# Query tiles' memory as a seventh place for gathered rows, and memory scores in three pieces

## What is computed

```
for each layer:
    mixer:   z = modulate(x) @ w_in, split into pool | q, kv (low rank) | memory q, k, v, gates
             attention: 8 heads, q = rms_norm(zq) @ w_uq, k, v = rms_norm(zkv) @ w_ukv
             memory, 4 heads, 2 directions: h = (q k^T * exp(gate terms)) v / max(|den|, exp(-m))
             x += gate * concat(pool, attention, memory) @ w_out
    PEER:    for each token: q = h @ w_q (8 heads x 2 halves of 128)
             s = q . subkeys  -> top 16 of 128 for both halves -> top 16 of the 256 sums
             g = softmax(best);  a = gelu(h . u_tab[expert])
             x += gate * sum over 8 x 16 experts of (g * a) * v_tab[expert]
context tokens pass only through the first layer's PEER; in layer 2 they give keys and values alone
```

## Time and profile before

| | us |
|---|---|
| median of 3 runs | 2786.68 |
| lowest, highest | 2786.67, 2791.87 |
| the profiled execution | 2789.06 |
| its span, first to last instruction | 2787.3 |

### The profile page before, as it was taken

How to read it: one execution, slowest core, us unless ns; L and a number is a source line. 1 busy time by engine, 2 the same in 40 slices (tenths; PEclk the granted TensorE clock), 3 DMA queues, 4 the chain that set the end, 5 groups by cost and what they waited for, 6 DMA issues and landing times.

```text
span 2787.3 us, 26625 instructions
## 1 busy us (share of the span) xinstructions
PE 2209.2 (79%) x8372; PEld 1037.6 (37%) x8372; DVE 1639.0 (59%) x4029; ACT 1121.3 (40%) x3259; POOL 813.1 (29%) x772
## 2 busy tenths in 40 slices
PE   7979899776777787787677777786799987777776
PEld 4747555332344343343122111175575321221111
DVE  2143567658786644676777666431525667776654
ACT  3132353545663433355333333332423343333333
POOL 0000233333354322334434333200003444343331
PEclk9869999778899889898899999995799999999999
DMA  7631599979999999999999999910016999999997
GB/s 316 235 123 36 217 404 406 358 275 393 395 387 421 421 420 421 412 420 421 422 421 421 421 421 421 372 71 30 16 37 242 424 425 426 425 426 426 426 426 309
DMA packets 133660, 940.05 MB, mean 337 GB/s; under 512 B 14864, under 2 KB 16144, under 8 KB 23312
## 3 DMA queue, kind: packets, MB, share of 16 engines
q0 software_dynamic: 110592, 805.36, 70.0%
q1 hardware_dynamic: 22496, 130.31, 11.9%
q10 hardware_dynamic: 432, 2.70, 0.3%
HBM read 937.26 MB, written 1.05 MB: 337 GB/s over the span
## 4 chain that ended last, share of the span: by engine, by line
DMA 45%; PE 31%; DVE 10%; ACT 10%; issue 3%; POOL 1%; SPq 0%; DVEq 0%; POOLq 0%; ACTq 0%
DMA fast<-uv_dram,idx 28%; DMA mix<-uv_dram,idx 16%; PE bank L1744 10%; PE bank L1703 4%; PE bank L1481 4%; DVE fast L1346 3%; PE bank L1667 2%; PE bank L1559 2%; ACT diag L921 1%; PE bank L1475 1%; ACT coef L918 1%; PE bank L1537 1%; PE bank L1651 1%; PE bank L1712 1%; ACT L917 1%
## 5 line engine op out<-in xcount | busy, mean ns | idle before, releaser
L1744 PE MATMUL bank<-fast,diag 128*64 128x512 f32 x2024 | 802.6, 664 | 294.5 <-ACT diag L921 292.7
L619 POOL DMA_INDIRECT fast<-uv_dram,idx x506 | 544.2, 1075 | 1497.5 <-PE bank L1744 778.5
L1346 DVE SCALAR_TENSOR_TENSOR fast<-fast,hrow 128x1024 f32<-128x1024 f32 x506 | 619.3, 1225 | 407.7 <-DMA fast<-uv_dram,idx 401.2
L917 ACT ACTIVATE gact<-araw 128x1 f32<-128x1 f32 x768 | 154.8, 202 | 1024.0 <-DVE fast L1346 645.0
L1744 PE MATMUL bank<-mix,diag 128*64 128x512 f32 x820 | 387.9, 630 | 120.9 <-ACT diag L921 119.3
L1744 PEld LDWEIGHTS bank<-fast,diag 128*64 128x64 f32 x2024 | 191.3, 145 | 762.0 <-ACT diag L921 513.6
L1346 DVE SCALAR_TENSOR_TENSOR mix<-mix,hrow 128x1024 f32<-128x1024 f32 x205 | 251.4, 1226 | 194.7 <-DMA mix<-uv_dram,idx 192.3
L619 POOL DMA_INDIRECT mix<-uv_dram,idx x205 | 206.4, 1007 | 327.5 <-PE bank L1744 306.1
L921 ACT ACTIVATE diag<-con,coef 128x64 f32<-128x64 f32 x768 | 267.1, 348 | 25.1
L918 ACT ACTIVATE coef<-gact,wts 128x1 f32<-128x1 f32 x768 | 226.2, 295 | 24.9
L1744 PEld LDWEIGHTS bank<-mix,diag 128*64 128x64 f32 x820 | 93.7, 140 | 370.0 <-ACT diag L921 250.3
(11 more groups left out here) (231 smaller groups left out, 2601.3 us busy)
## 6 DMA issues: line engine op xcount, KB each, us to landing
fast<-w_dram SPq DMA_DIRECT2D x48, 1024.0 KB, 7.2
back<-w_dram SPq DMA_DIRECT2D x44, 1024.0 KB, 10.4
qring<-wq_dram SPq DMA_DIRECT2D x40, 576.0 KB, 8.6
fast<-uv_dram,idx POOLq DMA_INDIRECT x506, 19.6
mix<-wq_dram SPq DMA_DIRECT2D x8, 576.0 KB, 6.3
mix<-uv_dram,idx POOLq DMA_INDIRECT x205, 26.3
fast<-uq_dram SPq DMA_DIRECT2D x4, 576.0 KB, 4.0
xT<-x_dram ACTq DMA_DIRECT2D x1, 2048.0 KB, 9.1
```

What stands on the lines that cost most here:

```text
L619: g.indirect_dma_start(slot(e, m), None, uv_tabs[e], bass.IndirectOffsetOnAxis(idx[:, Q % 2, n:n + 1], 0)).then_inc(landed[place], 16)
L917: link(a.activation(gact[:, n:n + 1], araw[:, Q % 2, n:n + 1], ACT.Gelu))
L1346: v.scalar_tensor_tensor(out=u, in0=u, scalar=1.0, in1=hrow[:, (2 * i + half) % 3, :], op0=ALU.mult, op1=ALU.mult, accum_out=araw[:, Q % 2 ...
L1744: mm = t_.matmul(acc[half, f * 512:(f + 1) * 512], diag[:, j % DIAGS, :], slot(e, j)[:, D + f * 512:D + (f + 1) * 512], start=(j % SLOTS < ...
```

## The change

Three edits:

1. A seventh place, `query`: the first 2048 columns of `qring`. It is open for slots 52 to 195, and its first gather waits for the key scores of units 0 to 15 (`psc_mm`). Units 16 and 17 are loaded at slot 196 instead of 41 and 49, after slot 195's values.
2. A memory unit's work on TensorE comes in three pieces. The gates' spreads and `st_mm` stay at slot 63 + 7h and wait, from the second unit on, for the exponentials of the unit before (`mE_ready`) instead of its weighting. The scores of the first two chunks come at +1, behind `mP_ready`, those of the other two at +2. A new signal `sc_mem` follows them, and VectorE's weighting of e = 0 waits for it.
3. The query norm's third square and its sum come two slots later (ScalarE at 45, TensorE at 47), and mean, root and scaling two slots later too (48, 49, 50).

```diff
-USES = (FAST_USES[0] + [("ctx", 0, 134, 266, "turned"), ("ctx", 0, 312, 512, "projected"),
+USES = (FAST_USES[0] + [("query", 0, 52, 196, "queried"), ("ctx", 0, 134, 266, "turned"), ("ctx", 0, 312, 512, "projected"),
...
+QUERY_FREE = 196
...
                 at = 10000 * e + ASKED[e][u - 2] + 2
+                if u in (HC, HC + 1):
+                    at = QUERY_FREE
...
+            if region == "query":
+                return qring[:, :, :, :].rearrange("p b k c -> p (b k c)")[:, 0:BIG]
...
+            if what == "queried":
+                return psc_mm, psc_mm.at(0, HC)
...
                     elif u >= 8:
+                        if u == HC:
+                            sp.wait_ge(v_used.sem, v_used.at(e, freed(e, QUERY_FREE - 1)))
                         sp.wait_ge(psc_mm.sem, psc_mm.at(e, u - 1))
...
                     for k in range(3):
+                        if k == 2:
+                            yield at + 3
                         square(p, KC + 2 + k, zqT[:, k, :])
-                    yield at + 5
+                    yield at + 7
                     root(p, 3)
...
-                    yield at + 4
+                    yield at + 6
                     mean(p, 3, KC + 5, QRANK)
-                    yield at + 6
+                    yield at + 8
                     inverse(p, 3)
...
                         v.wait_ge(mE_ready.sem, mE_ready.at(p, h + 1))
+                        if e == 0:
+                            v.wait_ge(sc_mem.sem, sc_mem.at(p, h + 1))
...
                     for k in range(3):
+                        if k == 2:
+                            yield in_at(group_of(p, "zq", 2) - 1) + 8
                         sum_square(p, KC + 2 + k, k == 0, k == 2)
...
             def memory_scores(p):
                 for h in range(MH):
-                    yield ML_AT + ML_STEP * h
+                    at = ML_AT + ML_STEP * h
+                    yield at
...
                     else:
-                        t_.wait_ge(mP_ready.sem, mP_ready.at(p, 2 * h))
-                    for kc in range(chunks(p)):
-                        mk = mkc if kc >= 2 or PHASES[p][1] else mkx
-                        t_.matmul(bank[kc // 2][:, kc % 2 * SEQ:kc % 2 * SEQ + SEQ], mk[f, c, kc % 2 * P:kc % 2 * P + P], mqT[f, c, :],
-                                  start=True, stop=True)
+                        t_.wait_ge(mE_ready.sem, mE_ready.at(p, h))
                     for e in range(DIRS):
...
                     mm.then_inc(st_mm.sem, 1)
+                    for j in range(chunks(p) // 2):
+                        yield at + 1 + j
+                        if h and j == 0:
+                            t_.wait_ge(mP_ready.sem, mP_ready.at(p, 2 * h))
+                        mk = mkc if j or PHASES[p][1] else mkx
+                        for kc in range(2):
+                            mm = t_.matmul(bank[j][:, kc * SEQ:kc * SEQ + SEQ], mk[f, c, kc * P:kc * P + P], mqT[f, c, :], start=True, stop=True)
+                    mm.then_inc(sc_mem.sem, 1)
```

More of the change, by code:

```diff
@@ L480, in build @@
         st_mm, marg_ready, mE_ready = signal("st_mm", *when(MH)), signal("marg_ready", *when(MH)), signal("mE_ready", *when(MH))
-        mP_ready = signal("mP_ready", *when(2 * MH))
+        mP_ready, sc_mem = signal("mP_ready", *when(2 * MH)), signal("sc_mem", *when(MH))
         num_mm, num_evac = signal("num_mm", *when(MH)), signal("num_evac", *when(MH))
```

## The result

The median of 4 runs is 2750.11 us (2737.53 to 2753.52), against 2789.0 (2786.67 to 2791.87) for the kernel before beside it: ratio 0.9852, 95% interval 0.9819 to 0.9885, 41 us of 2789. The direction was as forecast; the size is nearly twice the 21.1 us of the sum. A second set of 5 runs gave 2743.68 (2740.47 to 2753.2), ratio 0.9858 (0.9837 to 0.988).

The account below looks back on a forecast made before the run. Gather transfers were taken as the bound, with 51 us idle between 400 and 820 us. Terms 9.6 + 0.9 + 3.6 + 4.5 + 2.5 - 0 - 0 = 21.1 us off 2786.7 gave 2766 us, range 2750 to 2780.

Parts of the forecast that it names:

- A microsecond taken from that idle time moves every later gather: Idle transfer time in 400 to 820 us, 51 us in all: any saved is kept, since later gathers run at full rate.
- The pieces behind the experts: Four memory units, 510 to 615 us: with the spread first, the scores leave the chain, saving 9.6 us (5 to 11.3).
- The place: Seventh gather place: one more megabyte under way, worth 3.6 after unit 3, 4.5 in 615 to 745 us, 2.5 of run-ahead.
- the waits of the first slots after unit 3 for gathers gone: Sign expected in the changed profile; seven places would save 3.6 us (0 to 4.3) at slots 92 and 93.
- nothing of its own: In the memory units the chain holds no gather, so the seventh place alone gives nothing, only keeping gather waits off.
- the row stage: Stretch of 615 to 745 us: the place recovers half of 9.0 us idle transfer time, 4.5 us (0 to 9.0).
- the run-ahead behind it: After the attention, 745 to 820 us: transfers run one slot further ahead before the full-rate stretch, 2.5 us once (0 to 2.5).
- The queries' price: Loads of queries 16 and 17 move 2.8 us of transfers from 400 to 510 us into the full-rate stretch: taken as 0.
- The 0.9 us of the query norm: Moving the query's third square removes ScalarE's wait for TensorE's sums; worth 0 to 0.9 us, taken as 0.9.
- The place does little: Rival: where engines set the pace a free place gives nothing; 2 to 12 us gained, some 2779 us; chance 0.2.
- The clock comes back: Rival: in 510 to 615 us shorter waits keep TensorE at 2.4 GHz; 10 us more gained, 2756 us; chance 0.15.
- The clock goes: Rival: TensorE's grant falls to 0.66 in the attention and 400 to 510 us; 28 us slower, 2815 us; chance 0.04.

Follow-up runs that it names:

- pieces_m3: Memory scores in three pieces in mixer 3 alone, against the kernel before: 2776.43 us, ratio 0.9951.
- double_open: The changed kernel plus a second buffer for the odd units' masked scores in mixers 0 and 3: 2736.52 us, ratio 0.9828 to the kernel before.
- spread_first_unsplit: The changed kernel, but the scores follow the gates' spread in the same slot, not split: 2771.6 us, ratio 0.9953 to the kernel before.
- late_queries: The kernel before with queries 16 and 17 loaded after slot 195, their memory not used as a place: 2791.01 us, ratio 1.0022.
- zq_only: The kernel before with only the query norm's third square two slots later: 2788.38 us, ratio 1.0014.
- place_to_180: The changed kernel with the seventh place given back and the two queries loaded at slot 180, not 196: 2748.41 us, ratio 0.9871 to the kernel before.
- pieces_only: Memory scores in three pieces in mixers 0, 1 and 3, six places, query norm unchanged, against the kernel before: 2759.37 us, ratio 0.9897.
- pieces_m1: Memory scores in three pieces in mixer 1 alone, six places, against the kernel before: 2777.22 us, ratio 0.9959.
- place_pieces_m1: Seventh place, late query loads and pieces in mixer 1 only, query norm unchanged, against the kernel before: 2764.93 us, ratio 0.9922.
- no_zq: The changed kernel with the query norm as before, so place and pieces alone: 2745.44 us, ratio 0.9858 to the kernel before.

## Why the prediction was right and wrong

**The step that failed is the scope of the first part.** The prediction looks for the wait that counts "In 510 to 615 us, the four memory units", and costs the pieces for these, mixer 1's, alone; the sum has no term for mixers 0 and 3. The chain of mixer 3 would have given it by the same reading as the earlier trace rows: 3.71 us three times and 2.00 once, 13.1 us, and on a chain where nothing else competes. Measured: 12.9 us in the pair of traces, 13.7 by `pieces_m3`, and in the means of the traces 302.4 us for six kernels with the pieces in mixer 3 (`double_open` apart) against 315.9 for six without (`spread_first_unsplit` apart). Mixer 0 has the same code; the three together give 28.7 us, the two single ones 11.4 and 13.7, so it has 3.6 by difference, which the intervals don't separate from nothing. The traces lean the same way: the first dot comes at 310.0 us on average (307.1 to 312.5) in the seven kernels without pieces in mixer 0, and at 305.4 in the six with them (`spread_first_unsplit`, 306.0, apart). But these scatter from 301.5 to 313.4, and the 313.4 is after's own, so its trace shows 2.6 us lost where the others show a gain. The table of stretches was what misled: I looked for idle transfer time, and in mixers 0 and 3 there are hardly any transfers to be idle. "A microsecond taken from that idle time moves every later gather" was right, and so is its counterpart, which I did not ask: where no gather runs, what does the edit touch?

**The second failure is one of size, between slots 0 and 511.** The pair of traces gives 28.2 us there, and it isn't one odd execution: the four kernels without place and without pieces in mixer 1 (before, `pieces_m3`, `late_queries`, `zq_only`) take 1496.4 to 1502.3 us, the six with both take 1467.6 to 1471.7. The place alone takes 1480.5, the pieces 1484.7 and 1487.9: 18.1 and 12.3 us under the mean of neither, and both together 28.6. So nothing shows that one part strengthens the other, though the place alone is a single trace. By stretch, means or single values, with the range in brackets:

| us | neither | place | pieces | both | neither less both | forecast |
|---|---|---|---|---|---|---|
| 0 to 62 | 200.3 | 194.9 | 200.0, 199.6 | 197.7 (194.4 to 200.9) | 2.6 | 0.9 |
| 62 to 92 | 106.3 (102.7 to 109.0) | 99.7 | 93.5, 93.5 | 86.6 (84.7 to 88.5) | 19.7 | 9.6 + 3.6 |
| 92 to 128 | 107.6 (105.2 to 108.8) | 101.3 | 111.1, 108.1 | 101.8 (101.6 to 102.3) | 5.8 | 4.5 |
| 128 to 164 | 98.7 | 98.8 | 99.1, 99.1 | 99.1 | -0.3 | 0 |
| 164 to 196 | 89.9 | 87.5 | 89.8, 90.4 | 87.0 | 2.8 | 2.5 |
| 196 to 224 | 95.9 | 98.8 | 96.4, 95.2 | 98.8 | -2.9 | 0 |
| 224 to 511 | 799.2 | 799.5 | 798.0, 798.7 | 798.9 | 0.3 | 0 |

(`place_to_180` is left out of the rows of 164 and 196 under both, `late_queries` out of that of 196 under neither; under pieces stand `pieces_only` and `pieces_m1`.) The differences add up to 28 us. By the ratios the same two parts, with the pieces in mixer 1 only, give 21.7 us with an interval of 14 to 30, so the runs' times alone would not have shown this.

*The pieces behind the experts*: forecast 9.6 (5 to 11.3), measured 11.4 (8 to 15) by the ratios and 12.6 from the dot of slot 62 to that of 91 (next table). The forecast term holds the scores alone; what it leaves out is the level of the other instructions. Half a unit's numerators (14 instructions) take 1.78 us at the high level and 3.25 at the low one. The first six of the eight halves add up to 14.1 to 16.6 us in the four kernels with neither, 13.9 with the place alone, and 10.7 to 12.1 in all with pieces in mixer 1 (the last two halves are at the high level in all). From the mean of 15.2 to the 11.1 of `pieces_m1` that is 4.1 us, enough for the 3.0 that lie between 12.6 and 9.6; what of it was on the path wasn't isolated, so this cause is argued and not shown.

*The place*: forecast 10.6 in three terms, measured 7.8 (3 to 13) by the ratios, with the loads' cost in it. The border at slot 92 in the table above falls into a wait for a gather, and flatters the place in the row ahead of it: from the dot of slot 91 to that of 92 the kernels with six places take 5.1 to 5.5 us and those with seven about 1.1, but part of this comes back at the next dot, 3.4 to 4.1 against 4.1 to 4.6. VectorE still waits after unit 3 in after, one slot later: 3.11 us at slot 93 and 1.91 at slot 94, where before has 4.29 and 2.40 at slots 92 and 93.

```profile
600.13 1.23 DVE L1359 SCALAR_TENSOR_TENSOR fast<-fast,hrow 128x1024 f32<-128x1024 f32 x1 [3.11 <-DMA fast<-uv_dram,idx]
603.88 1.30 DVE L1359 SCALAR_TENSOR_TENSOR qring<-qring,hrow 128x1024 f32<-128x1024 f32 x1 [1.91 <-DMA qring<-uv_dram,idx]
```

So "the waits of the first slots after unit 3 for gathers gone" did not come true. With the borders at slots 91 and 96 the same kernels give:

| us | neither | place | pieces | both | neither less both | forecast |
|---|---|---|---|---|---|---|
| 62 to 91, the units | 100.9 (97.3 to 103.6) | 98.6 | 88.3, 88.4 | 85.5 (83.6 to 87.4) | 15.4 | 9.6 |
| 91 to 96 | 17.5 (17.2 to 17.9) | 14.3 | 16.8, 16.4 | 14.3 (13.9 to 14.8) | 3.2 | 3.6 |
| 96 to 128 | 95.6 (93.5 to 96.9) | 88.2 | 99.5, 96.8 | 88.7 (88.3 to 89.3) | 6.9 | 4.5 |

In the units the place alone stays within the scatter of neither, as the prediction's "nothing of its own" says; beside the pieces it brings 2.8 us there, as VectorE's waits for gathers shrink (22.4 us in `pieces_m1`, 9.6 + 3.4 in `place_pieces_m1`). Most of the excess over the forecast lies in this row, 15.4 us for 9.6. After unit 3 it brings the forecast amount. In the row stage it brings some 7 us, where the forecast took half of the 9.0 idle ones. The attention stretch doesn't move, and the run-ahead behind it is there, 2.8 for 2.5; both as the absence of gathers in the earlier trace rows said.

**The queries' price was mis-sized.** Taken as 0, bound 2.8; the loads cost 2.9 us in slots 196 to 224 (95.9 to 98.8 in the table), and `late_queries` is 6 us slower (2 to 11). My reason was that the 2.8 us they free in 400 to 510 us might be used there; in the trace that stretch moves at 406 GB/s, for 411 in the earlier trace rows, and `late_queries` takes 200.4 us from slot 0 to 62, where the other three with neither part take 200.0 to 200.5, so they were not. No wait of TensorE took the place: waits for query tiles from 880 to 1100 us are

```profile
PE bank L1723 <- DMA qring<-wq_dram: 3.5, 3, 1.7
```

in after and

```profile
PE bank L1703 <- DMA qring<-wq_dram: 4.2, 3, 1.7
```

in before. Gather 52 went out at 473.4 us, 0.7 later than in the earlier trace rows, and 1.8 earlier counted from each trace's first dot; it kept within the bound of 2.2. The 0.9 us of the query norm can't be seen: `zq_only` is 1.0014 (0.9997 to 1.003), and after is the same with and without it. That VectorE or the transfers end the stretch, and not TensorE's 0.90 us of waiting in the earlier trace rows, would explain it; no run tested it.

**The rivals.** "The place does little" fell: beside the pieces it brings 10 us by the ratios (11.4 to 21.7 with the pieces in mixer 1, and 28.7 to 39.6 from `pieces_only` to `no_zq`). "The clock comes back" came true in a small part. The grant of 510 to 615 us rose from 0.66 to 0.76 (in 510 to 596 us, up to slot 92, after has 0.75, its second execution 0.84, and the other kernels with both parts 0.71 to 0.80), and the numerators went to the high level as told; the values did not all follow: the pair at 527.67 us in after still takes 3.68, behind a wait of 5.14 us for ScalarE, and such waits were the argument against this rival. It was priced at 10 us for a full return; what the traces show of it are the 4.1 us of numerators above, of which it is open how much lay on the path. The rule in the Trainium skill ("TensorE: Matmul & The Clock Gate", HAM oscillation), that closing waits between bursts keeps the array fast, agrees with these numerators (3.25 to 1.78 us); with mixer 3 it doesn't, as the last section shows. "The clock goes" did not happen: 0.96, 0.90 and 0.98 for 0.98, 0.84 and 1.00.

**The sum, put right.** 28 us behind the experts in place of 21.1, and 13 in mixer 3 in place of 0, are 41 us; measured are 2789.0 - 2750.1 = 38.9 by the medians and 41 by the ratio. What mixer 0 may have gained is not in that sum.

What stays open: whether mixer 0 gained its 3.6 us, how much of the pieces' gain behind the experts is the clock's, and why slots 0 to 62 take 194.4 to 200.9 us with seven places, where they take 199.6 to 200.5 with six. The place opens in slot 52, so up to a few microseconds may be its own.

## What to carry to other kernels

Before costing an edit to a shared helper, list every place that calls it, and read the chain of waits at each one, above all where nothing overlaps it: there each microsecond counts in full. An instruction leaves the critical path only when everything that the waiting engine needs stands ahead of it in the same queue; putting it behind one of two such things gives nothing. And when a wait inside a TensorE-bound chain shrinks, price the chain's other instructions at both levels of the clock, since they may change level with it.

## What the runs showed of the hardware

TensorE's busy time alone did not decide the level of its clock. In mixer 3, memory units included, after has it busy for 61.3 of 75 us at a grant of 0.61 (columns as above):

```profile
1850.00:1925.00 75.00, 61.31 (x229) 49.52 (x228) 19.22 (x40) 18.99 (x44) 0.00 (x0) 0.61 0.11 39
```

and `double_open` for 65.4 at 0.66:

```profile
1850.00:1925.00 75.00, 65.41 (x230) 49.75 (x229) 28.43 (x59) 25.07 (x58) 0.00 (x0) 0.66 0.11 40
```

In the part of it where the chain holds TensorE and nothing else, it is busy for 35.6 of 36 us and has the lower level, a grant of 0.50, throughout:

```profile
1863.00:1899.00 36.00, 35.60 (x120) 29.11 (x120) 11.40 (x24) 10.95 (x28) 0.00 (x0) 0.50 0.00 0
```

The eight score instructions take 3.71 us there, the length of the 1.2 GHz level in the earlier trace rows, even in the units that start without a wait. So closing the waits didn't bring the clock back there, while behind the experts, where the same instructions stand between the experts' products, fewer waits and a higher level came together. What makes the difference is not settled by these runs.

Behind the experts the same work doesn't take the same time in each execution: in the four kernels with neither part in mixer 1, slots 62 to 92 took 102.7 to 109.0 us, the masks of the last two units lay 30.5, 25.9, 22.7 and 24.4 us apart, and the six halves of numerators named above took 14.1 to 16.6 us. A single trace's rows for that stretch carry some 6 us of this.
